# Who issues the modulation weight loads of the first feed-forward and the gate/up product: the GpSimd queue or the weights' queue (SyncE)

## The chip, the cores and the metric

One core of a Trainium2 chip runs the whole program. The metric is device microseconds of one launch. The profile is of one further execution; its times are microseconds from the start of the span. The engines are called PE (TensorE), DVE (VectorE), ACT (ScalarE), POOL (GpSimd) and SP (SyncE, which only issues DMAs here).

## The reference, cut to what matters

Two transformer blocks follow each other on one sequence of 256 tokens, D = 2048, all in float32. Each block has a modulation vector that is a product of one vector with a wide matrix, and the matrix products of a mixer and a feed-forward:

```
mod  = silu(c)   @ w_ada   + b_ada        # first block,  2048 x 12288
mod2 = silu(c_2) @ ada_w_2 + ada_b_2      # second block, 2048 x 12288
...
h = relu(u @ w_ff1)**2 ; y = h @ w_ff2    # first feed-forward,  D_FF = 8192
g = silu(u @ w_gate) * (u @ w_up)         # second one, gate and up, 5632 columns each
```

The modulation needs no TensorE: its matrices (100 MB each) are read chunk by chunk (512 columns) beside the large products and multiplied on DVE.

## The kernel before, in words

`phase_split_product` computes one large product. It runs in turns. In the two products that have an `entry` (first feed-forward, stream "ff_1": 8 turns; gate/up, stream "gate_up": 11 turns) one turn makes two chunks of 512 output columns, and each chunk takes four groups (q = 0 to 3 and q = 4 to 7), a group being four row tiles of weights, 1 MB. Products are exact in float32 by splitting: ACT rounds the weights to a high part (L1108), DVE subtracts it to get the low part (L1187), and PE multiplies high (L1286) and low (L1297).

**The weights' queue.** The ring of weights has two slots of one group, each loaded as two halves of 512 KB by SP (`refill`, L103). The half of group q is asked for when DVE's subtraction has used the same half of group q - 2 (semaphore `used`, raised behind L1187). `load_rest` (L125) is SP's loop over turns and groups.

**The modulation.** The class `Ada` (L195) reads one chunk of a modulation matrix per turn in eight loads of 512 KB (q = 0 to 7) into a ring of four slots that lies in `h_t`. A step (`step`, L254) multiplies one of 16 row tiles on DVE (L273 for the first two, L277 for the rest) and adds to `ada_sums`; behind step 15 one add, one transpose and one reduce follow (L282, L288, L291). A load feeds two steps, 2q and 2q + 1. Steps are laid between the subtractions: in turns from the second on they stand behind the halves of groups 1 to 6, in the proportion 16 steps to 12 places, so that step 14 and 15 stand behind the second half of group 6 and ahead of both subtractions of group 7. In the first turn all 16 stand in groups 4 to 6. In "gate_up" only turns 0 to 3 have steps, in "ff_1" all eight.

The loads are issued by POOL, which has nothing else to do in these phases: four at once, then each as soon as its slot is free (`load_when_free` waits until DVE has done the steps up to 2(q - 3) of that turn, counted by `ada_steps`).

**The end of a chunk.** Behind group 3 and behind group 7, ACT copies the low sums out (L866), DVE adds the high ones (L870), and PE may start the chunk after next in that bank. The first of a chunk's groups and the last are done column tile by column tile, so there PE wants all four row tiles of the group's low parts early; the other groups go row tile by row tile.

Of the kernel before, what the change touches and what calls it, by code (L numbers as in the profile page):

```python
# [22 lines left out]
RING = 2  # L23
# [27 lines left out]
class Chain:  # L51


    def __init__(self, sem):
        self.sem, self.n = sem, 0
# [47 lines left out]
def refill(sp, core, stream, i, q):  # L103

    src = stream.source(i, q)
    ring = core.rows_ring if stream.by_rows else core.ring
    slot, rows = q % RING, src.shape[1] // HALVES
    if isinstance(i, int):
        slot = (stream.first + stream.unit * i + q) % RING
    for half in range(HALVES):  # L110
        if not isinstance(i, int):
            sp.wait_ge(core.used, i * (HALVES * stream.unit) + (HALVES * (stream.first + q - RING) + half + 1))
        elif stream.first + stream.unit * i + q >= RING:
            sp.wait_ge(core.used, HALVES * (stream.first + stream.unit * i + q - RING) + half + 1)
        at = slice(half * rows, (half + 1) * rows)
        sp.dma_start(ring[:, slot, at, 0:src.shape[2]], src[:, at, :]).then_inc(core.landed[slot][half], 16)
# [5 lines left out]
        refill(sp, core, stream, g // stream.unit, g % stream.unit)  # L122


def load_rest(sp, core, stream):  # L125

    if stream.unit % RING == 0:
        with sp.Fori(0, stream.turns - 1) as i:
            for q in range(RING, stream.unit):
                refill(sp, core, stream, i, q)  # L130
            for q in range(RING):
                refill(sp, core, stream, i + 1, q)
        for q in range(RING, stream.unit):
            refill(sp, core, stream, stream.turns - 1, q)
    else:
        for g in range(RING, stream.groups):
            refill(sp, core, stream, g // stream.unit, g % stream.unit)
# [23 lines left out]
ASLOTS = 4  # L161
# [33 lines left out]
class Ada:  # L195
# [1 line left out]

    def __init__(self, ctx, nc, core, parts, turns, slots=ASLOTS, ring=None, acc=None, folded=True, rows=None):  # L200
# [7 lines left out]
        core.ada_landed_n[slots] += turns * self.per_slot  # L208
        core.ada_chunks += turns * self.per_turn
        sb = lambda name, shape: ctx.enter_context(nc.sbuf_tensor(name, shape, F32))  # L210
        self.ring = ring if ring is not None else sb(f"ada_weights_{self.chunks0}", [P, slots, AK, CW])
        self.acc = acc if acc is not None else sb(f"ada_sums_{self.chunks0}", [P, self.per_turn, 2, CW])
        if folded:
            self.folds0 = core.ada_folded
            core.ada_folded += turns * self.per_turn
            self.rows = (rows if rows is not None else
                         sb(f"ada_rows_{self.chunks0}", [P, turns * self.per_turn, NT * P // FOLD]))
            self.groups, at = [], 0
            for which in sorted({which for _, which, _, _ in self.parts}):
                firsts = [chunk0 for _, of, chunk0, _ in self.parts if of == which]  # L220
                self.groups.append((which, min(firsts), len(firsts) * turns, at))
                at += len(firsts) * turns
# [7 lines left out]
    def load(self, queue, i, q):  # L230
        w, _, chunk0, stride = self.parts[q // AGROUPS]
        queue.dma_start(self.ring[:, q % self.slots], w[:, q % AGROUPS, :, bass.ds((i * stride + chunk0) * CW, CW)]
                       ).then_inc(self.landed[q % self.slots], 16)

    def load_when_free(self, queue, i, q):

        steps = KT * self.per_turn
        queue.wait_ge(self.core.ada_steps, i * steps + (KT * self.chunks0 + AK * (q - self.slots + 1)))
        self.load(queue, i, q)

    def first_loads(self, queue):
        for q in range(self.slots):
            self.load(queue, 0, q)

    def other_loads(self, queue):
        n = self.per_turn * AGROUPS
        for load in range(self.slots, self.turns * n):
            self.load_when_free(queue, load // n, load % n)

    def multiply(self, dve, i):  # L250
# [3 lines left out]
    def step(self, dve, i, s):  # L254

        nc, core, n = self.nc, self.core, self.per_turn
# [7 lines left out]
                dve.wait_ge(core.ada_sums_taken, i * n + (self.chunks0 + 1))  # L264
        q = c * AGROUPS + k // AK
        if k % AK == 0:
            dve.wait_ge(self.landed[q % self.slots],
                        i * (16 * self.per_slot) + 16 * (self.landed0 + q // self.slots + 1))
# [721 lines left out]
def phase_split_product(nc, core, name, following, last_step, evictions=None, ada=None, ada_turns=None, entry=None,  # L990
# [7 lines left out]
    st = core.streams[name]  # L998
# [17 lines left out]
    with ExitStack() as ctx:  # L1016
        with_ada = (ada_turns or st.turns) if ada else 0
        ring = None if wide else core.hT[:].rearrange("p a b -> p (a b)").rearrange(
            "p (s k n) -> p s k n", s=ASLOTS, k=AK)
        ada = Ada(ctx, nc, core, ada, with_ada, ring=ring) if ada else None  # L1020
# [61 lines left out]

        @block.sync
        def _(sp):
            load_rest(sp, core, st)
            if following:
                prefetch(sp, core, core.streams[following])

# [265 lines left out]
        if ada:  # L1354
            @block.gpsimd
            def _(pool):
                if ring is not None:

                    pool.wait_ge(core.x_low, KT * (x0 + 1))
                ada.first_loads(pool)  # L1360
                ada.other_loads(pool)
    core.split_groups += st.groups
    core.split_phases += 0 if wide else 1
    core.tiles_ready_n += chunks * signals * st.turns
# [1934 lines left out]
def build(nc, t, out):  # L3299
    with ExitStack() as ctx:  # L3300
        core = Core()
        sb = lambda name, shape, dt=F32: ctx.enter_context(nc.sbuf_tensor(name, shape, dt))
        sem = lambda name: ctx.enter_context(nc.semaphore(name))
# [27 lines left out]
        core.norm_sems = [sem(n) for n in ("squares_ready", "sums_ready", "root_ready")]  # L3331
        core.scaled = sem("input_scaled")
        core.ada_landed = {n: [sem(f"ada_landed_{n}_{s}") for s in range(n)] for n in (IN_1_ASLOTS, ASLOTS, FIRST_ASLOTS)}
        core.ada_landed_n = {IN_1_ASLOTS: 0, ASLOTS: 0, FIRST_ASLOTS: 0}
        core.ada_steps, core.ada_sums_ready, core.ada_sums_taken = (
            sem(f"ada_{n}") for n in ("steps", "sums_ready", "sums_taken"))
# [6 lines left out]
        first = w_ada.rearrange("(g k p) n -> p g k n", p=P, k=KG)  # L3343
# [111 lines left out]
```

## Time and profile before

| what | us |
| --- | --- |
| median of three runs | 2905.76 (2901.91 to 2911.55) |
| the profiled execution, whole | 2904.72 |
| its span in the trace | 2903.0 |
| PE busy in the span | 2751.1 (95%) |
| DVE busy | 2061.6 (71%) |
| ACT busy | 1374.0 (47%) |
| POOL busy | 457.4 (16%) |

The profiled execution's own time is 1.7 us more than its span and 1.0 us less than the median. Stage "ff_1" runs from about 814 to 1192 us, "gate_up" from about 2117 to 2625 us. Busy shares are averages over the whole program; which engine sets the time must be read in each stage. In these two stages TensorE's granted clock is at or near its full level.

### The profile page before, as it was taken

The numbers are of one execution on the slowest core, as the hardware profiler recorded it, in microseconds if no ns is written. First come the engines' busy times: TensorE is split into PE (matmuls) and PEld (weight loads), VectorE is DVE, ScalarE is ACT, GpSimd is POOL, SyncE is SP. The second block draws the span as 40 slices with busy tenths as digits, with TensorE's granted clock in tenths as the row PEclk, the third lists the DMA queues.
The fourth block names the chain that finished last, engine by engine and source line by source line (L and its number), as shares of the span: only waits on it lengthen the run. The fifth ranks groups of instructions, "written<-read, shape, count | busy, mean of one in ns | idle before, by whom it ended". The sixth has DMA issues, their size and how long they took to land. (4 is left out here: it accounts for less than half of the span.)

```text
span 2903.0 us, 49916 instructions
## 1 busy us (share of the span) xinstructions
PE 2751.1 (95%) x19109; PEld 2538.8 (87%) x19109; DVE 2061.6 (71%) x2924; ACT 1374.0 (47%) x2210; POOL 457.4 (16%) x580
## 2 busy tenths in 40 slices
PE   8699999987989999999999999998989999999998
PEld 8689999886878888899998988887878888889998
DVE  6768996786787777787887678786577755555554
ACT  1354446534445555444544455455344444444454
POOL 1002998110011111111111021220011000000000
PEclk6799999998999999999999999999999999999999
DMA  9666666633657788788884666674568755555553
GB/s 386 237 209 241 216 218 197 211 105 130 237 196 273 270 276 277 259 279 282 264 280 134 175 232 221 204 239 135 186 218 279 243 189 186 180 189 166 176 190 129
DMA packets 290937, 632.43 MB, mean 218 GB/s; under 512 B 31490, under 2 KB 52422, under 8 KB 290502
## 3 DMA queue, kind: packets, MB, share of 16 engines
q1 hardware_dynamic: 239120, 484.78, 49.8%
q0 software_dynamic: 40192, 142.63, 14.6%
q10 hardware_dynamic: 11446, 2.54, 0.6%
q8 instruction: 123, 2.02, 0.3%
q14 instruction: 56, 0.46, 0.0%
HBM read 627.77 MB, written 2.10 MB: 217 GB/s over the span
## 5 line engine op out<-in xcount | busy, mean ns | idle before, releaser
L1187 DVE TENSOR_TENSOR weight_parts<-weights,weight_parts 128x1024 fp32r<-128x1024 f32 x584 | 706.9, 1222 | 295.7 <-ACT weight_parts L1108 294.6
L1108 ACT ACTIVATE weight_parts<-weights 128x1024 fp32r<-128x1024 f32 x584 | 607.2, 1057 | 557.0 <-PE accumulators L1297 240.4
L1286 PE MATMUL accumulators<-h_parts,weight_parts 128*128 128x512 f32 x2816 | 778.7, 398 | 20.6 <-DVE h_parts L1174 9.5
L1286 PEld LDWEIGHTS accumulators<-h_parts,weight_parts 128*128 128x128 f32 x2816 | 486.0, 190 | 90.5 <-DVE h_parts L1174 9.8
L1297 PEld LDWEIGHTS accumulators<-h_parts,weight_parts 128*128 128x128 f32 x2944 | 453.4, 190 | 71.0 <-DVE weight_parts L1187 10.5
L1297 PE MATMUL accumulators<-h_parts,weight_parts 128*128 128x256 f32 x2944 | 474.0, 283 | 6.8 <-DVE weight_parts L1187 6.5
L1332 PE MATMUL accumulators<-h_parts,weight_parts 128*128 128x256 f32 x1728 | 436.3, 284 | 1.8 <-DVE weight_parts L1187 1.8
L1334 PE MATMUL accumulators<-h_parts,weight_parts 128*128 128x256 f32 x1728 | 435.8, 284 | 0.0
L1332 PEld LDWEIGHTS accumulators<-h_parts,weight_parts 128*128 128x128 f32 x1728 | 334.1, 193 | 2.3 <-DVE weight_parts L1187 2.3
L1334 PEld LDWEIGHTS accumulators<-h_parts,weight_parts 128*128 128x128 f32 x1728 | 334.0, 193 | 0.0
L1328 PE MATMUL accumulators<-h_parts,weight_parts 128*128 128x256 f32 x1728 | 279.9, 285 | 8.9 <-ACT weight_parts L1108 8.9
L1652 PE MATMUL accumulators<-in_h_parts,in_weight_parts 128*128 128x256 f32 x1024 | 260.5, 287 | 22.9 <-DVE in_weight_parts L1973 22.8
L1654 PE MATMUL accumulators<-in_h_parts,in_weight_parts 128*128 128x256 f32 x1024 | 257.6, 284 | 0.0
L1812 ACT ACTIVATE in_weight_parts<-weights 128x512 fp32r<-128x512 f32 x256 | 157.2, 631 | 203.7 <-PE accumulators L1654 143.6
L1328 PEld LDWEIGHTS accumulators<-h_parts,weight_parts 128*128 128x128 f32 x1728 | 240.1, 193 | 9.3 <-ACT weight_parts L1108 9.3
L1973 DVE TENSOR_TENSOR in_weight_parts<-weights,in_weight_parts 128x512 fp32r<-128x512 f32 x256 | 187.6, 746 | 76.4 <-ACT in_weight_parts L1812 75.7
L2833 PE MATMUL accumulators<-in_h_parts,in_weight_parts 128*128 128x256 f32 x1632 | 216.9, 287 | 9.8 <-DVE in_weight_parts L3218 4.1
L2833 PEld LDWEIGHTS accumulators<-in_h_parts,in_weight_parts 128*128 128x128 f32 x1632 | 203.4, 192 | 21.1 <-issue 8.7
L1652 PEld LDWEIGHTS accumulators<-in_h_parts,in_weight_parts 128*128 128x128 f32 x1024 | 196.9, 192 | 27.6 <-DVE in_weight_parts L1973 27.3
L1654 PEld LDWEIGHTS accumulators<-in_h_parts,in_weight_parts 128*128 128x128 f32 x1024 | 197.2, 193 | 0.0
L2969 ACT ACTIVATE in_weight_parts<-weights 128x512 fp32r<-128x512 f32 (+6 forms) x224 | 120.9, 555 | 153.5 <-PE accumulators L2833 147.2
L3218 DVE TENSOR_TENSOR in_weight_parts<-weights,in_weight_parts 128x512 fp32r<-128x512 f32 (+6 forms) x224 | 129.7, 595 | 74.1 <-ACT in_weight_parts L2969 73.2
(404 smaller groups left out, 3497.3 us busy)
## 6 DMA issues: line engine op xcount, KB each, us to landing
weights<-in_w_ff SPq DMA_DIRECT2D x256, 512.0 KB, 5.4
weights<-in_w_in SPq DMA_DIRECT2D x160, 512.0 KB, 5.1
h_t<-in_ada_w POOLq DMA_DIRECT2D x96, 512.0 KB, 6.4
weights<-in_ffn_w_gate SPq DMA_DIRECT2D x88, 512.0 KB, 4.5
weights<-in_ffn_w_up SPq DMA_DIRECT2D x88, 512.0 KB, 4.6
weights<-in_ffn_w_down SPq DMA_DIRECT2D x88, 512.0 KB, 4.2
weights<-in_w_out SPq DMA_DIRECT2D x64, 512.0 KB, 4.7
wide<-in_ada_w POOLq DMA_DIRECT2D x128, 256.0 KB, 3.9
```

The costliest lines, as they stand in the source:

```text
L1108: nc.scalar.activation(w[:, held:held + take, 0, :], core.ring[:, q % RING, k:k + take, :], ACT.Copy).then_inc(core.high_ready, take)
L1187: ins = nc.vector.tensor_tensor(w[:, held:held + take, 1, :], core.ring[:, q % RING, k:k + take, :], w[:, held:held + take, 0, :].bitcast( ...
L1286: nc.tensor.matmul(core.ps[:, nt, :], high, x[:, kt].rearrange("p a t -> p (a t)"), start=(kt == 0), stop=False, skip_group_check=True)
L1297: ins = nc.tensor.matmul(rest(nt) if two else acc(c, nt), w[:, held, 1, nt * P:(nt + 1) * P], x[:, kt, 0, :], start=False, stop=(kt == KT ...
L1328: nc.tensor.matmul(accs[nt], w[:, held, 0, cols[nt]], xk[:, 0, :], start=(first and nt % 2 == 0), stop=False, skip_group_check=True)
L1332: nc.tensor.matmul(accs[nt], w[:, held, 0, cols[nt]], xk[:, 1, :], start=False, stop=False, skip_group_check=True)
L1334: ins = nc.tensor.matmul(accs[nt], w[:, held, 1, cols[nt]], xk[:, 0, :], start=False, stop=(last and nt % 2 == 1), skip_group_check=True)
L1652: nc.tensor.matmul(acc(c, nt), w[:, k, 0, nt * P:(nt + 1) * P], x[:, kt, 1, :], start=False, stop=False, skip_group_check=True)
L1654: ins = nc.tensor.matmul(acc(c, nt), w[:, k, 1, nt * P:(nt + 1) * P], x[:, kt, 0, :], start=False, stop=(kt == KT - 1 and nt % 2 == 1), sk ...
L1812: nc.scalar.activation(w[:, k, 0, :], core.ring[:, g % RING, part, :], ACT.Copy).then_inc(core.high_ready, 1)
L1973: ins = nc.vector.tensor_tensor(w[:, k, 1, :], core.ring[:, g % RING, part, :], w[:, k, 0, :].bitcast(F32), ALU.subtract)
L2833: ins = nc.tensor.matmul(out, stationary[:, a], moving[:, b], start=(kt == 0 and i == 0 and j == 0), stop=(kt == KT - 1 and i == 2 and j = ...
```

## The change

POOL now issues only the modulation loads of turn 0 of the two products with an `entry`. SP issues those of all later turns: the load q of turn i stands in SP's list right behind the weight refill of the same turn and the same q (both halves). The wait for a free slot is the same one, now done by SP. Landings of SP's loads are counted by four semaphores of their own (`ada_landed_by_sync`), and the DVE steps of turns from 1 on wait for those. SP's loop over turns is cut into pieces, since turn 0, the turns with modulation and those without have different bodies. Other phases are as before.

```diff
-def load_rest(sp, core, stream):
+def load_rest(sp, core, stream, ada=None, ada_turns=0):
+    def loads(i, groups, with_ada):
+        for q in groups:
+            refill(sp, core, stream, i, q)
+            if with_ada:
+                ada.load_when_free(sp, i, q, core.ada_landed_by_sync)
+    def turns(first, end, with_ada, next_with_ada):
+        if first < end:
+            with sp.Fori(first, end) as i:
+                loads(i, range(RING, stream.unit), with_ada)
+                loads(i + 1, range(RING), next_with_ada)
+    last = stream.turns - 1
     if stream.unit % RING == 0:
-        with sp.Fori(0, stream.turns - 1) as i:
...
+        if ada:
+            turns(0, 1, False, True)
+            turns(1, min(ada_turns - 1, last), True, True)
+            if ada_turns <= last:
+                turns(ada_turns - 1, ada_turns, True, False)
+                turns(ada_turns, last, False, False)
+        else:
+            turns(0, last, False, False)
+        loads(last, range(RING, stream.unit), ada is not None and ada_turns == stream.turns)
...
-    def load_when_free(self, queue, i, q):
+    def load_when_free(self, queue, i, q, landed=None):
         steps = KT * self.per_turn
         queue.wait_ge(self.core.ada_steps, i * steps + (KT * self.chunks0 + AK * (q - self.slots + 1)))
-        self.load(queue, i, q)
+        self.load(queue, i, q, landed)
...
         if k % AK == 0:
+            if self.by_sync and not (isinstance(i, int) and i == 0):
+                dve.wait_ge(self.core.ada_landed_by_sync[q % self.slots],
+                            i * (16 * self.per_slot) + 16 * (self.sync0 + q // self.slots + 1 - self.per_slot))
+            else:
...
-            load_rest(sp, core, st)
+            load_rest(sp, core, st, ada if entry else None, with_ada)
...
-                ada.other_loads(pool)
+                ada.other_loads(pool, 1 if entry else None)
```

## Rows read from the trace of the kernel before

**Rows 1.** The page's busy part, and windows of stage ff_1 and of gate_up without modulation.
```profile
PE 2751.1 (95%) x19109; PEld 2538.8 (87%) x19109; DVE 2061.6 (71%) x2924; ACT 1374.0 (47%) x2210; POOL 457.4 (16%) x580
...
core 0: us, PE busy (x) PEld busy (x) DVE busy (x) ACT busy (x) POOL busy (x), PEclk, DMA share, GB/s
890.00:950.00 60.00, 60.00 (x344) 52.43 (x343) 44.53 (x58) 33.97 (x59) 7.36 (x11) 1.00 0.82 286
2310.00:2350.00 40.00, 40.00 (x231) 35.01 (x230) 20.96 (x24) 18.75 (x24) 0.00 (x0) 1.00 0.58 186
```

**Rows 2.** Timeline of ACT: ends of chunks in ff_1 (L909), of turns in gate_up (L960).
```profile
943.49 1.33 ACT L909 ACTIVATE ff_sums<-ff_sums 128x256 f32<-128x256 f32 x4
...
989.34 1.33 ACT L909 ACTIVATE ff_sums<-ff_sums 128x256 f32<-128x256 f32 x4
...
1056.70 1.40 ACT L909 ACTIVATE ff_sums<-ff_sums 128x256 f32<-128x256 f32 x4
...
1079.70 1.33 ACT L909 ACTIVATE ff_sums<-ff_sums 128x256 f32<-128x256 f32 x4
...
2286.82 1.33 ACT L960 ACTIVATE gate<-gate 128x256 f32<-128x256 f32 x4
2332.10 1.33 ACT L960 ACTIVATE gate<-gate 128x256 f32<-128x256 f32 x4
2377.00 1.33 ACT L960 ACTIVATE gate<-gate 128x256 f32<-128x256 f32 x4
```

**Rows 3.** Timeline of PE: idle time in turn 0 and at a chunk's end.
```profile
867.29 0.60 PE L1297 MATMUL accumulators<-h_parts,weight_parts 128*128 128x256 f32 x2 [2.22 <-DVE weight_parts L1187]
...
966.33 1.18 PE L1286 MATMUL accumulators<-h_parts,weight_parts 128*128 128x512 f32 x4 [0.70 <-DVE ff_sums L870]
```

**Rows 4.** Waits of 830 to 1260 us: total, times, longest.
```profile
ACT weight_parts L1108 <- DMA weights<-in_w_ff: 111.2, 56, 4.9
...
DVE ada_sums L277 <- DMA h_t<-in_ada_w: 2.1, 2, 1.9
```

**Rows 5.** Timeline of DVE, one turn of ff_1: group 5's second half to group 7.
```profile
995.35 1.22 DVE L1187 TENSOR_TENSOR weight_parts<-weights,weight_parts 128x1024 fp32r<-128x1024 f32 x1
...
1000.09 1.41 DVE L277 SCALAR_TENSOR_TENSOR ada_sums<-h_t,c_act,ada_sums 128x512 f32<-128x512 f32 x2
1001.53 0.69 DVE L282 TENSOR_TENSOR ada_sums<-ada_sums 128x512 f32<-128x512 f32 x1
...
1003.71 3.49 DVE L1187 TENSOR_TENSOR weight_parts<-weights,weight_parts 128x1024 fp32r<-128x1024 f32 x3
```

**Rows 6.** Timeline of PE: group 7's first low products in that turn.
```profile
1006.63 0.64 PE L1297 MATMUL accumulators<-h_parts,weight_parts 128*128 128x256 f32 x4
```

**Rows 7.** Timeline of POOL (that turn's load q = 7), and L232 from 890 to 1150.
```profile
984.30 0.72 POOL L232 DMA_DIRECT2D h_t<-in_ada_w  x1 [3.98 <-DVE ada_sums L277]
...
L232 POOL DMA_DIRECT2D h_t<-in_ada_w x45: 724/724/724, 893.6 to 1137.0; - x45
```

**Rows 8.** L116 (SP's refills): one issue in that turn; landings from 890 to 1150.
```profile
L116 SPq DMA_DIRECT2D weights<-in_w_ff x1: 373/373/373, 996.7 to 996.7; - x1
...
DMA to landing us min/median/max: 3.6/5.4/9.0
```

**Rows 9.** Three loads in a row on SP's queue, 306 to 308.5 us: L232, L116.
```profile
L232 SPq DMA_DIRECT2D wide<-in_w_ada x1: 379/379/379, 306.1 to 306.1; - x1
...
DMA to landing us min/median/max: 3.9/3.9/3.9
...
L116 SPq DMA_DIRECT2D weights<-in_w_in x2: 327/327/327, 306.7 to 307.5; - x2
...
DMA to landing us min/median/max: 5.0/5.3/5.5
```

**Rows 10.** Timelines of DVE and of PE, the same places of a turn in gate_up.
```profile
2246.70 1.22 DVE L1187 TENSOR_TENSOR weight_parts<-weights,weight_parts 128x1024 fp32r<-128x1024 f32 x1
...
2251.43 1.41 DVE L277 SCALAR_TENSOR_TENSOR ada_sums<-h_t,c_act,ada_sums 128x512 f32<-128x512 f32 x2
...
2259.20 0.64 PE L1297 MATMUL accumulators<-h_parts,weight_parts 128*128 128x256 f32 x4
```

More of the change, by code:

```diff
@@ L122, in prefetch @@
         refill(sp, core, stream, g // stream.unit, g % stream.unit)
-def load_rest(sp, core, stream):
-    if stream.unit % RING == 0:
-        with sp.Fori(0, stream.turns - 1) as i:
[L129 to L134, printed above, removed]
+def load_rest(sp, core, stream, ada=None, ada_turns=0):
[10 more added lines that the diff above has]
+    last = stream.turns - 1
+    if stream.unit % RING == 0:
+        if ada:
[7 more added lines that the diff above has]
+        loads(last, range(RING, stream.unit), ada is not None and ada_turns == stream.turns)
     else:
@@ L195, with __init__ @@
 class Ada:
-    def __init__(self, ctx, nc, core, parts, turns, slots=ASLOTS, ring=None, acc=None, folded=True, rows=None):
+    def __init__(self, ctx, nc, core, parts, turns, slots=ASLOTS, ring=None, acc=None, folded=True, rows=None,
+                 by_sync=False):
+        self.by_sync, self.sync0 = by_sync, core.ada_synced
         self.slots, self.landed, self.folded = slots, core.ada_landed[slots], folded
@@ L207, in __init__ @@
         self.landed0, self.chunks0 = core.ada_landed_n[slots], core.ada_chunks
-        core.ada_landed_n[slots] += turns * self.per_slot
+        core.ada_synced += (turns - 1) * self.per_slot if by_sync else 0
+        core.ada_landed_n[slots] += (1 if by_sync else turns) * self.per_slot
         core.ada_chunks += turns * self.per_turn
@@ L228, in row, with load @@
         return i * stride + (at + chunk0 - first)
-    def load(self, queue, i, q):
+    def load(self, queue, i, q, landed=None):
         w, _, chunk0, stride = self.parts[q // AGROUPS]
         queue.dma_start(self.ring[:, q % self.slots], w[:, q % AGROUPS, :, bass.ds((i * stride + chunk0) * CW, CW)]
-                       ).then_inc(self.landed[q % self.slots], 16)
-    def load_when_free(self, queue, i, q):
+                       ).then_inc((landed or self.landed)[q % self.slots], 16)
+    def load_when_free(self, queue, i, q, landed=None):
         steps = KT * self.per_turn
         queue.wait_ge(self.core.ada_steps, i * steps + (KT * self.chunks0 + AK * (q - self.slots + 1)))
-        self.load(queue, i, q)
+        self.load(queue, i, q, landed)
     def first_loads(self, queue):
@@ L243, in first_loads, with other_loads @@
             self.load(queue, 0, q)
-    def other_loads(self, queue):
+    def other_loads(self, queue, turns=None):
         n = self.per_turn * AGROUPS
-        for load in range(self.slots, self.turns * n):
+        for load in range(self.slots, (turns or self.turns) * n):
             self.load_when_free(queue, load // n, load % n)
@@ L266, in step @@
         if k % AK == 0:
-            dve.wait_ge(self.landed[q % self.slots],
-                        i * (16 * self.per_slot) + 16 * (self.landed0 + q // self.slots + 1))
+            if self.by_sync and not (isinstance(i, int) and i == 0):
+                dve.wait_ge(self.core.ada_landed_by_sync[q % self.slots],
+                            i * (16 * self.per_slot) + 16 * (self.sync0 + q // self.slots + 1 - self.per_slot))
+            else:
+                dve.wait_ge(self.landed[q % self.slots],
+                            i * (16 * self.per_slot) + 16 * (self.landed0 + q // self.slots + 1))
         w = self.ring[:, q % self.slots, k % AK, :]
@@ L1019, in phase_split_product @@
             "p (s k n) -> p s k n", s=ASLOTS, k=AK)
-        ada = Ada(ctx, nc, core, ada, with_ada, ring=ring) if ada else None
+        ada = Ada(ctx, nc, core, ada, with_ada, ring=ring, by_sync=entry is not None) if ada else None
         x = ctx.enter_context(nc.sbuf_tensor(f"h_parts_{g0}", [P, depth if wide else KT, 2, SEQ], F32R))
@@ L3333, in build @@
         core.ada_landed = {n: [sem(f"ada_landed_{n}_{s}") for s in range(n)] for n in (IN_1_ASLOTS, ASLOTS, FIRST_ASLOTS)}
+        core.ada_landed_by_sync, core.ada_synced = [sem(f"ada_landed_by_sync_{s}") for s in range(ASLOTS)], 0
         core.ada_landed_n = {IN_1_ASLOTS: 0, ASLOTS: 0, FIRST_ASLOTS: 0}
```

## The prediction

> **What bounds the kernel now.** I read the page's busy part first, then windows of the two stages that the diff touches, then the ends of chunks one by one. PE is busy 95% of the span, and in a window of ff_1 60.00 of 60 us at the full granted clock; DVE is at 44.53 of 60, and the DMA engines at 0.82 of their time [rows 1]. In gate_up behind the modulation turns PE is also at 40.00 of 40, with the DMA share at only 0.58 [rows 1]. So PE sets the pace with the modulation beside it and without. The ends of chunks say how exactly. A turn without modulation takes 2377.00 - 2332.10 = 44.90 us [rows 2], half a turn 22.45. In ff_1 two half turns run from 943.49 to 989.34, 45.85 us instead of 44.90, and one from 1056.70 to 1079.70, 23.00 instead of 22.45 [rows 2]; the other half turns behind turn 0 are at 22.40 to 22.46. In gate_up one modulation turn takes 45.28 (2286.82 to 2332.10) [rows 2], the other full ones 44.91. What the modulation turns behind turn 0 lose to anything but PE is therefore 0.95 + 0.55 + 0.38 = 1.9 us in all. The first of these shows where it comes from: PE idle 0.70 us, waiting for DVE's eviction of the chunk [rows 3], which was late because its subtractions had waited for weights that had not landed. ACT waited 111.2 us for landings in ff_1, at most 4.9 at a time [rows 4]; nearly all of it is swallowed by the two groups that ACT and DVE run ahead of PE.
>
> **What the change removes.** POOL's issues go: 7 x 8 in ff_1, 3 x 8 in gate_up, each 724 ns [rows 7]. POOL has nothing else here, so that is worth nothing by itself. What can be won is the 1.9 us: before, POOL's loads of a turn come in bunches, just where weights are wanted; behind the change there is one load of 512 KB with every two halves, evenly spread. I take all of the 1.9 as won; the other end is nothing.
>
> The Trainium skill, SBUF — State Buffer, the box "The 'DVE blocks DMA' trap" in the section "SBUF: two separate sides", says that a DVE operation that takes the port pair shared with GpSimd keeps GpSimd from writing its descriptors, and that a load issued from SP is free of this. Here all 45 POOL issues of ff_1 show 724 ns, minimum and maximum alike [rows 7], so the issue itself shows no such wait; the descriptors behind it the trace does not show. By that rule loads would land earlier on SP, which moves nothing beyond what is priced above.
>
> **What it adds on SP.** 24 issues a turn instead of 16, at about 0.37 us each [rows 8]: 8.9 of 44.9 us. The added wait for a free slot never holds SP up, by the order of DVE's list: load q of turn i wants the steps up to 2(q - 3). For q = 4 to 7 these (2, 4, 6, 8 steps) stand behind groups 1, 2 (first half), 3 (first half) and 3, while SP gets there only when the second half of group q - 2 (2, 3, 4, 5) is subtracted; for q = 0 to 3 they are 10, 12, 14 and 16 steps of the turn before, done in its groups 4 to 6, while SP comes behind groups 6, 7, 0 and 1. So nothing queues behind it: the refills stay as early as they are, price 0. If SP did stand still, each microsecond would first eat the lead of some two groups.
>
> **What it moves, and this is the step that costs.** The load is no longer issued when its slot is free, but behind the refill of its own q, and that waits for DVE. For seven of the eight loads there is room: load 6 goes out behind group 4 and is used behind group 5's second half, with the chunk's eviction between (about 9.6 us); the others have that or more. Load 7 has not. Before, it was issued at 984.30 and used by step 14 at 1000.09 [rows 5, 7]: 15.8 us. Behind the change it waits for the second subtraction of group 5, which starts at 995.35 and takes 1.22 [rows 5]. SP's issue of the refill follows at 996.7 [rows 8], and the modulation load behind it at about 997.2 (0.373 for the issue, about 0.1 for registers). Step 14 wants it at 1000.09, 2.9 us later, and the fastest landing of any refill in ff_1 is 3.6 us [rows 8]. So DVE must wait, in every turn from 1 on.
>
> How long: the refill ahead of it lands some 3.5 us behind its issue, since with POOL's loads gone its queue is empty then; the load lands one transfer later. Three loads issued in a row landed at 306.1 + 3.9 = 310.0, at 306.7 + 5.0 = 311.7 and at 307.5 + 5.5 = 313.0 [rows 9]: 1.3 to 1.7 us apart. I take 996.7 + 3.5 + 1.7 = 1001.9, a wait of 1.8 us. From below: 3.6 behind 997.2 is 1000.8, a wait of 0.7. From above: a landing at the 9.0 that ff_1 also shows [rows 8] is 1006.2, a wait of 6.1. The empty queue makes me stay near the lower end.
>
> Behind the waiting step in DVE's list stand steps 14 and 15, the add, the transpose, the reduce, and the two subtractions of group 7. Today the second of those ends at 1003.71 + two thirds of 3.49 = 1006.04 [rows 5]. PE's first low products of group 7 start at 1006.63, the ones of row tile 2 0.27 later, and their weight load 0.2 before [rows 6]: they want it by 1006.7. The slack is 0.65 us, and PE stands for the rest: 1.8 - 0.65 = 1.15 us. It comes back every turn, since DVE and ACT take their next start from PE's end of chunk. The two lost microsecond parts of today don't add to it: group 7's end shifts with PE, so the eviction has more room, not less. ff_1 has 7 such turns: 7 x 1.15 = 8.1 us.
>
> In gate_up the eviction is shorter and DVE earlier. Its second subtraction of group 5 starts at 2246.70, step 14 at 2251.43, 4.73 apart as in ff_1 (1000.09 - 995.35 = 4.74), so the wait is 1.8 again; but step 14 stands 7.77 us ahead of the low products (2259.20) instead of 6.54 (1006.63) [rows 5, 6, 10]. The slack is 0.65 + 1.23 = 1.9, just more than the wait: 3 turns x 0. With a landing 1 us later it would be 3 x 0.9.
>
> **The sum.** 2904.7 - 1.9 + 8.1 = 2910.9; against the median of the runs, 1.0 above the profiled one, the same step of 6.2 us gives 2912. I say 2911, 0.2% above. Turn 0's stall of 2.22 us [rows 3] I leave as it is: there 16 steps stand in three groups and DVE is full; its loads stay with POOL.
>
> The Trainium skill, DMA: Bandwidth & Descriptors, section "SWDGE vs HWDGE vs iDMA", says that an SDMA engine keeps loads issued by GpSimd and by SP in different internal queues and takes turns between them. By that, load 7 loses its own turn when it goes behind the refill in SP's queue; it would land before the refill's end if both queues were used. That is the side my 1.7 us stands on, and no row here compares the two directly.
>
> **Rivals.**
> - Only the relief (the load lands inside the slack). It needs a landing by 1000.09 + 0.65, 3.5 us behind the load's issue with another load just ahead. Then 2904.7 - 1.9 = 2902.8. For it: alone, loads land in 3.6; against it: rows 9. Chance 0.15.
> - More relief: turn 0's stall goes too, because the four POOL loads for turn 1 no longer share its last groups. Then 1.9 + 2.2 in ff_1 + as much in gate_up = 6.3 less: 2898.4. Against it: DVE's list in turn 0 is the same. This is the case on the other side; it decides only if that wait is a landing's. Chance 0.06.
> - Queueing: the refill of group 7 and load 7 find the loads before them still under way, as today's weights do at up to 9.0. A landing at 7.5 behind the refill's issue gives a wait of 4.1, 3.5 on PE in 7 turns and 2.2 in 3: 24.5 + 6.6 - 1.9 = 29, 2934. For it: the share of 0.82 [rows 1]; against: the spread loads. Chance 0.12.
> - SP is held up in a way that the code doesn't show (the pieces of its loop, the issue of 24 loads): refills late by 1 to 2 us in several turns, another 5 to 15 us on the sum, 2920. Chance 0.07. That the slot wait bites is the same case; its order excludes it.
>
> **How the numbers follow.** The forecast's case has 0.60, its own range 2905 to 2918 (waits from 1.2 to 2.7 in ff_1). Within 0.3% is 8.7 us to either side of 2905.8, about what a measurement can tell from no change. Slower by more: a third of the forecast's case (0.20), the queueing case whole, two thirds of SP's: 0.36. Faster by more: 0.05, most of the second rival. Within: 0.59. The range takes the relief in and leaves most of the queueing out: 2900 to 2922.
>
> **What would show it.** In the changed trace: SP issues h_t loads, 56 and 24; the wait of DVE L277 for DMA h_t grows from 2.1 us [rows 4] to some 7 x 1.8 + 3 x 1.8 = 18, once a turn; PE idles about 1.1 us before L1297 at the start of group 7 of ff_1's turns, released by L1187; ends of turns in ff_1 46.0 apart, in gate_up 44.9; ACT's waits for weights in ff_1 well under 111 us. Wrong if DVE does not wait there, if the wait stands elsewhere, or if ff_1's turns are at 44.9.

## The result and the profile after

The changed kernel is slower: median 2919.93 us of 7 runs (2913.27 to 2924.33), the kernel before 2905.4 us of 7 (2901.82 to 2911.55); ratio 1.0049, interval 1.0036 to 1.0063, which is 10 to 18 us. The forecast was 2911, range 2900 to 2922: the place and the mechanism were as written, the loss, 14.5 us, is two to three times the 5 to 6 us forecast. The ratios and intervals in this document are those of the record, not the quotients of the medians given; the two differ by up to 0.001, less than the intervals reach to either side. One of ff1_only's twelve runs, 4419.58 us at a granted clock of 0.55, is counted as a slow one and left out of its ratio.

The page of the changed kernel, its busy part; then its waits from 830 to 1260 us (total, times, longest) and, behind the dots, from 2150 to 2320. Helper lines have moved: L250 issues the modulation loads, L299 is the step, L1209 the low subtraction, L1308 and L1319 the high and low products.

```profile
span 2916.0 us, 49962 instructions
## 1 busy us (share of the span) xinstructions
PE 2756.4 (95%) x19109; PEld 2537.6 (87%) x19109; DVE 2060.9 (71%) x2924; ACT 1375.1 (47%) x2210; POOL 401.1 (14%) x500
```

```profile
ACT weight_parts L1130 <- DMA weights<-in_w_ff: 85.4, 50, 3.9
...
DVE ada_sums L299 <- DMA h_t<-in_ada_w: 17.3, 9, 2.9
PEld accumulators L1319 <- DVE weight_parts L1209: 17.2, 18, 2.7
...
DVE ada_sums L299 <- DMA h_t<-in_ada_w: 7.6, 5, 2.1
```

POOL has 80 instructions fewer: the 56 and 24 loads. PE's busy time is 5.3 us up, its idle time in the span 7.7 us. ACT waits less for weights (85.4 against 111.2 us [rows 4]), and DVE waits more for modulation loads, 17.3 against 2.1 us in the same window.

Where in a turn: the DVE timeline of the changed kernel over the stretch of a turn that [rows 5] show, from group 5's second subtraction to group 7's.

```profile
999.37 1.22 DVE L1209 TENSOR_TENSOR weight_parts<-weights,weight_parts 128x1024 fp32r<-128x1024 f32 x1
1000.51 0.74 DVE L299 SCALAR_TENSOR_TENSOR ada_sums<-h_t,c_act,ada_sums 128x512 f32<-128x512 f32 x1
...
1002.97 1.22 DVE L1209 TENSOR_TENSOR weight_parts<-weights,weight_parts 128x1024 fp32r<-128x1024 f32 x1
1006.48 1.41 DVE L299 SCALAR_TENSOR_TENSOR ada_sums<-h_t,c_act,ada_sums 128x512 f32<-128x512 f32 x2 [2.29 <-DMA h_t<-in_ada_w]
...
1010.10 4.62 DVE L1209 TENSOR_TENSOR weight_parts<-weights,weight_parts 128x1024 fp32r<-128x1024 f32 x4
```

And PE at group 7 of that turn, where [rows 6] show it without idle time:

```profile
1009.73 1.09 PE L1308 MATMUL accumulators<-h_parts,weight_parts 128*128 128x512 f32 x4
1011.37 0.50 PE L1319 MATMUL accumulators<-h_parts,weight_parts 128*128 128x256 f32 x2 [0.55 <-DVE weight_parts L1209]
1012.51 0.51 PE L1319 MATMUL accumulators<-h_parts,weight_parts 128*128 128x256 f32 x2 [0.63 <-DVE weight_parts L1209]
```

The pair of idle times comes back in ff_1's turns 1 to 6 (0.54 to 1.12 us, then 0.63), and in turn 7 one of the two (0.64). The two short idle times add to less than what the turn loses, since the ends of products are modelled; the ends of chunks tell the loss better. Here they are for ACT in the changed kernel, a half turn apart:

```profile
970.91 1.33 ACT L931 ACTIVATE ff_sums<-ff_sums 128x256 f32<-128x256 f32 x4
...
993.37 1.33 ACT L931 ACTIVATE ff_sums<-ff_sums 128x256 f32<-128x256 f32 x4
...
1017.53 1.33 ACT L931 ACTIVATE ff_sums<-ff_sums 128x256 f32<-128x256 f32 x4
```

22.46 us to the end of group 3, as ever, and 24.16 to the end of group 7. Why the wait is 2.3 us and not 1.8, SP's list tells (the changed kernel, the refill of group 7's second half and load 7 behind it in this turn, each with its landing):

```profile
L116 SPq DMA_DIRECT2D weights<-in_w_ff x1: 373/373/373, 1000.8 to 1000.8; - x1
...
DMA to landing us min/median/max: 4.3/4.3/4.3
...
L250 SPq DMA_DIRECT2D h_t<-in_ada_w x1: 372/372/372, 1001.4 to 1001.4; - x1
...
DMA to landing us min/median/max: 5.0/5.0/5.0
```

The refill lands at 1005.1, load 7 at 1006.4, 1.3 us later; DVE starts at 1006.48.

The seven turns differ, and the difference is the best evidence for the mechanism. DVE's waits in turns 1 to 7 are 2.50, 2.41, 2.29, 2.85, 2.28, 2.45 and 1.68 us; the half turns around them take 1.93, 1.82, 1.71, 2.27, 1.70, 1.87 and 1.02 us more than 22.45. Wait less loss is 0.57 to 0.59 us in the first six and 0.66 in the last: each microsecond of wait beyond a slack of 0.6 is one on PE.

**A ledger by stages.** Single executions differ by some us in stages that the change does not touch: the changed kernel's ff_1 had its first chunk's end 3.6 us later in the span than the kernel before. So each kernel is read by three stretches of its own profiled execution: the second half of ff_1's turn 0; ff_1's turns 1 to 7, from that chunk's end to the last one's; and gate_up, from the first chunk's end of turn 0 to that of turn 10. For the kernel before the first two come from these ACT rows, and gate_up from L960 in the same way:

```profile
846.30 1.33 ACT L909 ACTIVATE ff_sums<-ff_sums 128x256 f32<-128x256 f32 x4
...
876.13 1.33 ACT L909 ACTIVATE ff_sums<-ff_sums 128x256 f32<-128x256 f32 x4
...
1191.70 1.32 ACT L909 ACTIVATE ff_sums<-ff_sums 128x256 f32<-128x256 f32 x4
```

| kernel | turn 0, second half | ff_1, turns 1 to 7 | gate_up | ratio to before, interval |
| --- | --- | --- | --- | --- |
| before | 29.83 | 315.57 | 453.23 | |
| changed | 27.45 | 326.57 | 455.41 | 1.0049 (1.0036 to 1.0063) |
| early7 | 27.12 | 314.35 | 452.75 | 0.9985 (0.9971 to 0.9999) |
| early_all | 28.70 | 314.34 | 453.76 | 0.9994 (0.9983 to 1.0006) |
| ff1_only | 27.52 | 326.38 | 453.40 | 1.0034 (1.0022 to 1.0046) |
| gate_only | 27.78 | 315.84 | 455.62 | 0.9992 (0.9981 to 1.0003) |
| pool_late | 26.79 | 325.00 | 453.72 | 1.0041 (1.0026 to 1.0056) |
| steps_to_7 | 23.23 | 314.93 | 449.65 | 0.9975 (0.9965 to 0.9985) |
| pool_steps_to_7 | 23.23 | 315.16 | 449.15 | 0.9973 (0.9961 to 0.9984) |
| best | 23.37 | 314.92 | 448.98 | 0.9976 (0.9966 to 0.9986) |
| late7 | 27.80 | 367.43 | 474.12 | 1.0262 (1.0244 to 1.0280) |

For the changed kernel 11.0 us lie in ff_1's turns 1 to 7. Gate_up has 2.2 more, of which 1.8 are in turn 0 and 0.35 in the turns whose loads SP issues. Turn 0 takes 1 to 3 us more or less in executions of kernels that are alike there, and the granted clock accounts for most of it: DVE's stall makes PE idle, and PE then runs for some time at half its clock, the lower of its two levels, 1.2 GHz. The windows of PE in the kernel before around the stall of [rows 3] (us from:to, length, busy time of PE, PEld, DVE, ACT and POOL, granted clock, DMA share, GB/s), and behind the dots the window of steps_to_7 in which PE idles in the same half turn:

```profile
864.00:867.00 3.00, 1.07 (x6) 0.54 (x4) 2.93 (x4) 1.07 (x2) 0.72 (x1) 1.00 1.05 407
867.00:870.00 3.00, 2.17 (x7) 1.68 (x8) 2.51 (x3) 0.05 (x1) 0.00 (x0) 0.59 1.01 382
870.00:873.00 3.00, 3.00 (x11) 2.52 (x10) 1.89 (x3) 1.67 (x3) 0.00 (x0) 0.50 1.05 387
873.00:876.00 3.00, 3.00 (x16) 2.68 (x15) 0.42 (x1) 0.54 (x2) 0.00 (x0) 0.77 0.82 268
...
873.00:877.00 4.00, 2.83 (x18) 2.27 (x16) 3.97 (x6) 1.19 (x4) 0.00 (x0) 1.00 0.77 261
```

By an estimate, one less the granted clock summed over windows of 1 us, the missing clock is worth 3.4 us in ff_1's turn 0 of the kernel before and 1.7 in the changed one; in gate_up's turn 0 it is 1.7 and 3.4, the other way round. So the 1.8 us of gate_up's turn 0, and most of what ff_1's turn 0 seems to win, come with this clock. Whether the change has a part in it, one execution each can't tell; gate_only, also at 3.4 in gate_up, is over its runs no slower than the kernel before. Besides, the turns of gate_up without modulation take 44.80 us in some executions and 44.90 in others, 0.6 us in its column, which no run explains.

### The profile page after: what moved, and what is told of

The parts are those of the page before. It is cut to its first block and busy times, and to the rows that moved or that the text cites. A ratio compares the mean times of both kernels' runs of the same rounds, so it can differ in the third digit from the quotient of the medians.

```text
span 2916.0 us, 49962 instructions
## 1 busy us (share of the span) xinstructions
PE 2756.4 (95%) x19109; PEld 2537.6 (87%) x19109; DVE 2060.9 (71%) x2924; ACT 1375.1 (47%) x2210; POOL 401.1 (14%) x500
## 3 DMA queue, kind: packets, MB, share of 16 engines
q0 software_dynamic: 28672, 100.68, 10.5%
## 5 line engine op out<-in xcount | busy, mean ns | idle before, releaser
L1209 DVE TENSOR_TENSOR weight_parts<-weights,weight_parts 128x1024 fp32r<-128x1024 f32 x584 | 704.8, 1220 | 272.2 <-ACT weight_parts L1130 270.9
L1308 PE MATMUL accumulators<-h_parts,weight_parts 128*128 128x512 f32 x2816 | 777.9, 398 | 20.6 <-DVE h_parts L1196 9.4
L1308 PEld LDWEIGHTS accumulators<-h_parts,weight_parts 128*128 128x128 f32 x2816 | 485.6, 190 | 90.4 <-DVE h_parts L869 10.1
L1319 PEld LDWEIGHTS accumulators<-h_parts,weight_parts 128*128 128x128 f32 x2944 | 452.8, 190 | 83.4 <-DVE weight_parts L1209 23.6
L1319 PE MATMUL accumulators<-h_parts,weight_parts 128*128 128x256 f32 x2944 | 476.1, 283 | 16.0 <-DVE weight_parts L1209 15.9
L1674 PE MATMUL accumulators<-in_h_parts,in_weight_parts 128*128 128x256 f32 x1024 | 263.6, 289 | 19.0 <-DVE in_weight_parts L1995 18.8
L1676 PE MATMUL accumulators<-in_h_parts,in_weight_parts 128*128 128x256 f32 x1024 | 260.8, 286 | 0.0
L2855 PE MATMUL accumulators<-in_h_parts,in_weight_parts 128*128 128x256 f32 x1632 | 217.7, 288 | 10.5 <-DVE in_weight_parts L3240 5.0
L2855 PEld LDWEIGHTS accumulators<-in_h_parts,in_weight_parts 128*128 128x128 f32 x1632 | 204.1, 193 | 22.2 <-issue 9.1
L1674 PEld LDWEIGHTS accumulators<-in_h_parts,in_weight_parts 128*128 128x128 f32 x1024 | 199.7, 195 | 23.6 <-DVE in_weight_parts L1995 23.4
L1676 PEld LDWEIGHTS accumulators<-in_h_parts,in_weight_parts 128*128 128x128 f32 x1024 | 199.8, 195 | 0.0
L1667 PE MATMUL accumulators<-in_h_parts,in_weight_parts 128*128 128x256 f32 x1024 | 177.9, 297 | 3.7 <-DVE in_h_parts L1865 3.7
```

The source lines that it names most:

```text
L1209: ins = nc.vector.tensor_tensor(w[:, held:held + take, 1, :], core.ring[:, q % RING, k:k + take, :], w[:, held:held + take, 0, :].bitcast( ...
L1308: nc.tensor.matmul(core.ps[:, nt, :], high, x[:, kt].rearrange("p a t -> p (a t)"), start=(kt == 0), stop=False, skip_group_check=True)
L1319: ins = nc.tensor.matmul(rest(nt) if two else acc(c, nt), w[:, held, 1, nt * P:(nt + 1) * P], x[:, kt, 0, :], start=False, stop=(kt == KT ...
L1667: nc.tensor.matmul(acc(c, nt), w[:, k, 0, nt * P:(nt + 1) * P], x[:, kt, 0, :], start=(kt == 0 and nt % 2 == 0), stop=False, skip_group_ch ...
L1674: nc.tensor.matmul(acc(c, nt), w[:, k, 0, nt * P:(nt + 1) * P], x[:, kt, 1, :], start=False, stop=False, skip_group_check=True)
L1676: ins = nc.tensor.matmul(acc(c, nt), w[:, k, 1, nt * P:(nt + 1) * P], x[:, kt, 0, :], start=False, stop=(kt == KT - 1 and nt % 2 == 1), sk ...
```

## The experiments

Each was timed in five rounds beside the kernel before (late7 in three). The diffs are against the changed kernel where nothing else is said.

### early7: one load of eight, one refill earlier

```diff
             refill(sp, core, stream, i, q)
             if with_ada:
-                ada.load_when_free(sp, i, q, core.ada_landed_by_sync)
+                for n in {6: (6, 7), 7: ()}.get(q, (q,)):
+                    ada.load_when_free(sp, i, n, core.ada_landed_by_sync)
```

> The changed kernel, with one load of the eight moved: load 7 of a turn stands behind the refill of group 6 instead of group 7 (SP issues it some 9 us before its use, not 2.9); loads 0 to 6 and the number of loads on SP are as in the changed kernel. Theory 1 (the whole loss is the wait of step 14 for load 7): DVE's wait for h_t loads falls from 23 us to under 4, the half turns of ff_1 that take 24.1 to 24.7 us go back to 22.4 to 22.6, and the time to within 3 us of the kernel before, ratio to it 1.000 (0.999 to 1.001). Theory 2 (SP's queue carries 24 loads of 512 KB a turn and the weights land later for it): DVE's wait goes but PE still waits for subtractions at group 7, and at least half of the 14 us stays, ratio 1.0025 or more.

Measured: 2907.16 us against 2908.69, ratio 0.9985 (0.9971 to 0.9999). DVE's waits for modulation loads in ff_1, of which there is one, in turn 0, and the same stretch of a turn:

```profile
DVE ada_sums L300 <- DMA h_t<-in_ada_w: 0.7, 1, 0.7
```

```profile
1005.05 1.22 DVE L1210 TENSOR_TENSOR weight_parts<-weights,weight_parts 128x1024 fp32r<-128x1024 f32 x1
1006.19 1.41 DVE L300 SCALAR_TENSOR_TENSOR ada_sums<-h_t,c_act,ada_sums 128x512 f32<-128x512 f32 x2
```

Steps 14 and 15 follow the subtraction at once, and all half turns of ff_1 behind turn 0 take 22.45 or 22.46 us: 314.35 for turns 1 to 7, 12.2 less than in the changed kernel and 1.2 less than before. So load 7 alone is the loss. Theory 2 falls: with the same 24 loads a turn on SP's queue PE waits for nothing. The ratio lies below the 0.999 to 1.001 expected; by the medians it is 0.9995, and the interval reaches almost to 1, so that early7 is faster than the kernel before is not shown.

### early_all: every load one refill earlier

```diff
             refill(sp, core, stream, i, q)
-            if with_ada:
-                ada.load_when_free(sp, i, q, core.ada_landed_by_sync)
+            if q + 1 < stream.unit:
+                if with_ada:
+                    ada.load_when_free(sp, i, q + 1, core.ada_landed_by_sync)
+            elif next_with_ada:
+                ada.load_when_free(sp, i + 1, 0, core.ada_landed_by_sync)
```

> The changed kernel, with all modulation loads on SP one refill earlier: load q+1 behind the refill of group q. Theory 1: as with load 7 alone, no wait of DVE for h_t loads over 0.5 us in turns from 1 on, ratio to the kernel before 0.999 to 1.001. The spread loads could also give back the 1.9 us that the turns lost before: then 0.9993. Theory 2 (the weights' landings are what costs): ratio 1.0025 or more.

Measured: 2908.12 against 2908.69, ratio 0.9994 (0.9983 to 1.0006); ff_1's turns 1 to 7 at 314.34, the same as early7. It confirms, and shows that for the other seven loads neither place matters.

### ff1_only and gate_only: the change in one stage

```diff
-        ada = Ada(ctx, nc, core, ada, with_ada, ring=ring, by_sync=entry is not None) if ada else None
+        ada = Ada(ctx, nc, core, ada, with_ada, ring=ring, by_sync=name == "ff_1") if ada else None
...
-            load_rest(sp, core, st, ada if entry else None, with_ada)
+            load_rest(sp, core, st, ada if name == "ff_1" else None, with_ada)
...
-                ada.other_loads(pool, 1 if entry else None)
+                ada.other_loads(pool, 1 if name == "ff_1" else None)
```

(gate_only has "gate_up" in the three places.)

> SP issues the loads of turns from 1 on in ff_1 alone; gate_up is as before. Theory 1: 7 turns at 1.75 us less the 1.5 us that ff_1 lost before, 10 to 12 us over the kernel before, ratio 1.0035 to 1.0045; nearly all of the change's loss. Rival (the loss is the same in each turn of both stages, 14 us over 10 turns): 10 us, so this run alone does not decide, its partner does.

> SP issues the loads of turns from 1 on in gate_up alone (3 turns); ff_1 is as before. Theory 1: DVE waits some 2 us a turn there too but PE's slack of 1.9 us swallows it: 0 to 1 us, ratio 1.000 to 1.0005. Rival (the same loss in each turn): 3 turns at 1.4 to 1.75 us, 4 to 5 us, ratio 1.0015 or more.

Measured: ff1_only 2918.54 against 2908.69 (2918.18 without the run of 4419.58), ratio 1.0034 (1.0022 to 1.0046), a hair under the stretch given, ff_1's turns at 326.38; gate_only 2907.42, ratio 0.9992 (0.9981 to 1.0003), where 1.000 to 1.0005 was expected; the interval holds 1. The loss is ff_1's, though DVE waits in gate_up too: in the changed kernel 1.94, 2.13 and 1.58 us in its three turns, with PE losing 0.35 us in all (0.5 in gate_only). The rival of an equal loss per turn falls; the slack of 1.9 us that the prediction gave that stage is what the runs show.

### pool_late: the old queue, the new moment

Against the kernel before:

```diff
         for load in range(self.slots, self.turns * n):
+            if paced_by and load >= n:
+                queue.wait_ge(self.core.used, HALVES * (paced_by.first + load - RING + 1))
             self.load_when_free(queue, load // n, load % n)
```

> The kernel before (POOL issues all modulation loads), with one more wait ahead of each load of turns from 1 on: the same count of used weights behind which SP issues it in the changed kernel. So the time of issue is the changed kernel's, the queue is the old one. Theory 1 (the time of issue is what costs): DVE waits 2 to 3.5 us at step 14 of each turn, PE loses 1.5 to 3 us in ff_1's seven turns, 12 to 22 us in all, ratio 1.004 to 1.0075. Rival (the place in SP's queue behind a refill costs, and a queue of its own is served at once): the load lands 1 to 1.5 us sooner, waits under 1 us, ratio under 1.0015.

Measured: 2916.65 against 2906.13, ratio 1.0041 (1.0026 to 1.0056). The DVE row of one turn, and POOL's issue of that load 7 with its landing:

```profile
952.23 1.22 DVE L1189 TENSOR_TENSOR weight_parts<-weights,weight_parts 128x1024 fp32r<-128x1024 f32 x1
...
959.04 1.42 DVE L279 SCALAR_TENSOR_TENSOR ada_sums<-h_t,c_act,ada_sums 128x512 f32<-128x512 f32 x2 [1.99 <-DMA h_t<-in_ada_w]
```

```profile
L232 POOL DMA_DIRECT2D h_t<-in_ada_w x1: 722/722/722, 953.7 to 953.7; - x1
...
DMA to landing us min/median/max: 5.2/5.2/5.2
```

ff_1's turns 1 to 7 take 325.0 us, 9.4 over the kernel before; the changed kernel has 11.0 over it. So the moment of issue is 86% of the loss, and who issues at most the rest, 0.2 us a turn. The seven waits at step 14 are 1.9 to 2.6 us, 2.1 in the mean against 2.35 in the changed kernel, and wait less loss is 0.56 to 0.66 us again. The rival asked for a wait under 1 us. The ratio lies within the expectation at its lower end, the 10.5 us between the medians just below its 12 to 22.

From the trigger (952.23 + 1.22) to step 14 it is 5.6 us by POOL, and 5.9 by SP (999.37 + 1.22 to 1006.48). But POOL's load goes out 0.3 us behind the trigger and SP's 0.8 (0.4 in the last turn), since SP issues the refill first; from issue to landing POOL's take 5.1 to 5.8 us in the seven turns and SP's 4.8 to 5.6. The Trainium skill, DMA: Bandwidth & Descriptors, section "SWDGE vs HWDGE vs iDMA", says that the two kinds of queue take turns in a DMA engine. These runs show no gain from that: POOL's load lands earlier by less than it is issued earlier, and what the turns between queues are worth stays open.

### steps_to_7, pool_steps_to_7 and best: no urgent work behind the wait

```diff
             def sums(i, q, k, with_sums):
                 start = 4 if entry and isinstance(i, int) and i == 0 else 1
-                if with_sums and start <= q < st.unit - 1:
-                    n, slots, at = (ada.per_turn * KT, KG * (st.unit - 1 - start) // take,
+                end = st.unit if entry else st.unit - 1
+                if with_sums and start <= q < end:
+                    n, slots, at = (ada.per_turn * KT, KG * (end - start) // take,
```

The same edit on the kernel before is pool_steps_to_7, and on early_all it is best.

> The changed kernel, with DVE's 16 steps laid over groups 1 to 7 instead of 1 to 6 (in turn 0 over groups 4 to 7) in the two products with an entry. The loads and their place in SP's queue are the same; load 7 is then used behind group 7's second half, some 4.5 us later, and nothing that PE wants soon stands behind it. Theory 1: no wait or a harmless one, ff_1's half turns back at 22.4 to 22.6, and in turn 0 of both stages some of the stall of 2.8 us goes too: 3 us over to 6 us under the kernel before, ratio 0.998 to 1.001. Theory 2 (SP's queue delays the weights): ratio 1.0025 or more.

> The kernel before with the same new lay of DVE's steps (over groups 1 to 7, in turn 0 over 4 to 7); POOL issues all modulation loads. It says what that lay gives by itself. Expected: the stalls of turn 0 (2.8 to 3.5 us in each of the two stages) shrink to under 1 us, the rest is as before: 2 to 6 us less, ratio 0.998 to 0.9993. If the last steps now delay the eviction at a turn's end, it is 0 to 5 us slower instead.

> The changed kernel with both repairs: each modulation load one refill earlier on SP, and DVE's steps over groups 1 to 7 (turn 0: 4 to 7). Expected: no wait of DVE for h_t in turns from 1 on, smaller stalls in turn 0, evenly spread loads: 3 to 8 us under the kernel before, ratio 0.997 to 0.999. If the queue of the loads matters apart from their time, it differs from the same lay with POOL's loads by more than 2 us.

Measured: steps_to_7 2898.32, pool_steps_to_7 2897.13, best 2899.43, against 2906.13: ratios 0.9975, 0.9973 and 0.9976, each with an interval of 0.001 to either side. Best is within its expectation; steps_to_7 (0.998 to 1.001) and pool_steps_to_7 (0.998 to 0.9993) are faster than theirs, by more than was said: 7.8 and 9.0 us between the medians, where at most 6 was expected. In steps_to_7 the step stands behind group 7's second subtraction and finds its load landed:

```profile
1003.62 1.23 DVE L1209 TENSOR_TENSOR weight_parts<-weights,weight_parts 128x1024 fp32r<-128x1024 f32 x1 [1.18 <-ACT weight_parts L1130]
1004.76 1.41 DVE L299 SCALAR_TENSOR_TENSOR ada_sums<-h_t,c_act,ada_sums 128x512 f32<-128x512 f32 x2
```

Three things follow. With load 7 at the changed kernel's place in SP's list but used 8.4 us behind its trigger instead of 3.6, the loss is gone (314.93). The lay of the steps is worth 7 to 9 us by itself, nearly all of it in the two turns 0: ff_1's second half falls to 23.23 us from 27 to 30, gate_up's total by 4 us, since 16 steps now stand in four groups instead of three. Two things go there at once: in ff_1 PE's idle time in that half turn falls from 2.5 to 2.9 us in two stalls to 1.1 to 1.3 in one, and the granted clock stays at 1.00, which by the same estimate gives back 1.7 or 3.4 us more; the expectations had priced the idle time alone. And who issues the loads makes no difference that these runs can tell: the three kernels are within 0.0003 of each other. By the medians best is 2.3 us over pool_steps_to_7, a little more than the 2 us that the expectation named as the sign that the queue matters, but that is less than the intervals, 3 us to either side, can tell. All three beat both the kernel before and the changed one; the simplest of them keeps POOL's loads.

### late7: a larger dose

```diff
             refill(sp, core, stream, i, q)
-            if with_ada:
+            if load_7_of is not None and q == 0:
+                ada.load_when_free(sp, load_7_of, 7, core.ada_landed_by_sync)
+            if with_ada and (q < 7 or i is last):
                 ada.load_when_free(sp, i, q, core.ada_landed_by_sync)
```

> The changed kernel with load 7 later still: behind the refill of group 0 of the next turn, about 3.6 us after its place in the changed kernel (the two subtractions of group 6 and the step between them lie in between); in ff_1's last turn, which has no next one, it stays. A dose for the slack. Theory 1 (each microsecond by which load 7 lands beyond the slack is one on PE, once a turn; slack 0.6 us in ff_1, 1.9 in gate_up): DVE waits about 6 us in ff_1's turns 1 to 6 and about 5.5 in gate_up's 1 to 3; PE loses 5.3 in ff_1's six turns, 1.5 in the seventh, and 3.6 in each of the three of gate_up: 44 us over the kernel before, ratio 1.015 (1.012 to 1.018). Rival (PE's two groups of lead take up part of it, the loss saturates): under 25 us, ratio under 1.009.

Measured: 2980.82 against 2906.47, ratio 1.0262 (1.0244 to 1.0280): 74 us over, where 44 were expected. The loss does not saturate; it is more than linear. The DVE row of one turn of late7, then PE's timeline and windows, as above:

```profile
971.09 1.41 DVE L301 SCALAR_TENSOR_TENSOR ada_sums<-h_t,c_act,ada_sums 128x512 f32<-128x512 f32 x2 [7.60 <-DMA h_t<-in_ada_w]
```

```profile
975.97 0.80 PE L1321 MATMUL accumulators<-h_parts,weight_parts 128*128 128x256 f32 x2 [5.86 <-DVE weight_parts L1211]
977.11 0.80 PE L1321 MATMUL accumulators<-h_parts,weight_parts 128*128 128x256 f32 x2 [0.34 <-DVE weight_parts L1211]
977.70 1.91 PE L1310 MATMUL accumulators<-h_parts,weight_parts 128*128 128x512 f32 x4
...
980.26 1.91 PE L1310 MATMUL accumulators<-h_parts,weight_parts 128*128 128x512 f32 x4
...
982.71 1.08 PE L1310 MATMUL accumulators<-h_parts,weight_parts 128*128 128x512 f32 x4
...
984.09 1.09 PE L1310 MATMUL accumulators<-h_parts,weight_parts 128*128 128x512 f32 x4
```

```profile
970.00:976.00 6.00, 0.14 (x2) 0.03 (x1) 4.71 (x7) 0.34 (x1) 0.00 (x0) 0.69 0.09 34
976.00:979.00 3.00, 2.66 (x8) 2.08 (x9) 3.00 (x3) 0.38 (x1) 0.00 (x0) 0.50 0.57 158
979.00:982.00 3.00, 3.00 (x11) 2.52 (x10) 1.08 (x3) 0.38 (x1) 0.00 (x0) 0.50 1.02 358
982.00:985.00 3.00, 3.00 (x17) 2.69 (x16) 0.71 (x2) 1.09 (x4) 0.00 (x0) 0.91 1.04 395
```

Two sizes were off. DVE waits 7.6 us, not 6: the load goes out 3.6 us later behind group 5's subtraction than in the changed kernel, as meant, but in line behind both halves of the next refill, and takes 6.7 us to land, not 5. The six waits are 7.1 to 7.6 us. And PE, idle for 5.9 us, comes back at half its clock: the granted clock is 0.50, the lower of its two levels, 1.2 GHz, and the next two column tiles start 2.56 and 2.45 us apart instead of 1.40, 2.2 us lost. Together 7.6 - 0.6 + 2.2 = 9.2 us; the six half turns concerned lose 7.8 to 9.5, 8.6 in the mean, and gate_up's three turns lose 6.0 to 8.0, where 3.6 was expected. In the changed kernel PE's idle time at this place is 1.2 to 1.8 us in turns 1 to 6 and the granted clock stays at 1.00, so this term was absent there. The Trainium skill, TensorE: Matmul & The Clock Gate, section "Part 1: The HAM clock gate", names the same two levels and puts the drop to the lower one down to idle time; the trace agrees, here behind 5.9 us and in the kernel before's turn 0 behind 2.22 us of idle time.

## Why the prediction was right, and where its sizes were off

- **PE sets the pace; landings of weights are swallowed.** Right. ACT's waits for weights changed from 111 to 85 us and little followed from it (1.2 us, below); the half turns without a late load are at 22.39 to 22.46.
- **Turns behind turn 0 lose 1.9 us before, to be won.** Two thirds right. Of the three parts the 0.95 and 0.55 us in ff_1 are gone in early7 and early_all (turns 1 to 7 at 314.3 against 315.57), 1.2 us by that stretch. The third, 0.38 us in gate_up, was misread: the turn that takes 45.28 us does so in early7, steps_to_7 and ff1_only too. It is the last turn with steps, and PE, which does not idle in it, there does small products that sum the rows (8 in the trace, 0.26 us), work of its own that no load changes.
- **SP's slot wait never bites, 24 issues cost nothing.** Right by early7 and best: SP issues as many loads and waits on the same counts. In the changed kernel SP waited for a free slot three times between 880 and 1200 us, 0.8 us in all.
- **Load 7 is the one that moves from 15.8 us ahead to 2.9.** Right in place and turn: one wait a turn, at step 14, in all ten turns.
- **DVE waits 1.8 us.** This is the mis-sized term. It measured 1.7 to 2.9 us in ff_1's seven turns, 2.35 in the mean. The spacing behind the refill was about right (1.2 to 2.1 us for 1.7); the refill itself was put at 3.5 us, the landing on an empty queue, and took 3.9 to 4.5. The queue is not empty: in the turn shown the refill's first half went out 2.5 us before it, at 998.3, and landed at 1002.2, 1.4 us after the second half's issue.
- **The slack is 0.65 us in ff_1 and 1.9 in gate_up.** Right in ff_1: 2.41 us of waiting cost a half turn 24.27 - 22.45 = 1.82, so 0.6 was slack, and the other turns say the same. Right in gate_up: waits of 1.6 to 2.1 us cost 0.35 in three turns, and wait less loss is 1.8 to 1.9 in the two that lost something.
- **The sum.** 7 x 1.15 = 8.1 us was forecast; seven half turns lost 1.0 to 2.3 us, 1.75 in the mean, 12.2 in all (326.57 - 314.35). Less the 1.2 won, the stretch is 11.0 longer. With the measured wait the prediction's own sum is 7 x 1.7 - 1.5 = 10.4, which the interval of 10 to 18 us holds. The median lies at 14.5 and the stages explain 11; the gap is within the interval, and turn 0's clock alone moves an execution by 1.7 us in either stage. No further mechanism showed. That the range held is in part luck: the median of 2919.93 lies above the 2905 to 2918 of the forecast's own case, whose upper end leaves out what a wait of 2.7 us costs gate_up by the prediction's own slack (3 x 0.8 = 2.4), and inside the 2922 that stood for other cases too.
- **Turn 0 stays.** Its stall is DVE's, as written (in ff_1 a longest idle time of PE of 1.9 to 2.3 us in the traces whose steps stand in three groups; where they stand in four it is gone, and 1.1 to 1.3 us of waiting for the eviction are left, 1.4 to 1.6 in gate_up). The prediction took 2.22 us as its whole size. With the second idle time and the half clock behind it, ff_1's second half of turn 0 is 4.3 to 7.4 us over 22.45 and gate_up's turn 0 3.2 to 5.6 over 44.90; this is where the time of this code lies.
- **The rival of queueing** had a germ of truth in size (landings of 5 us and more), none in extent: at 12% it stood for landings 7.5 us behind the refill, and the changed kernel's seven turns show 5.2 to 6.2.

## What to carry to other kernels

A load that is moved behind a trigger is safe only if the time from the trigger to its use, read off the consumer's list, exceeds a landing on a busy queue, less the slack of what stands behind the use; check every load of the cycle, because one of eight can fail alone. What a late load costs is its wait less the slack of whatever stands behind the waiting instruction in the same list, once per turn, and more once TensorE's granted clock falls; moving the load forward by one trigger or the use back behind the urgent work cured it equally here. Look at the granted clock of a stall before pricing it: by the estimate above the stalls of turn 0 cost 1.7 or 3.4 us more than their idle time in every profiled execution with steps in three groups, but for one, early7's gate_up. Who issues a load mattered 0.2 us a turn here, and when it was issued 1.3 us or more.

## What the runs showed of the hardware

- Loads of 512 KB issued 0.6 us apart on SP's queue landed 1.2 to 2.1 us apart in ff_1's turns 1 to 6 of the changed kernel. There, between 890 and 1150 us at a DMA share of 0.80, landings took 5.4 us in the median for weights and 6.0 for the modulation, where the fastest took 3.7.
- Behind the same trigger a load by GpSimd landed 0.2 us sooner than by SP in the mean of seven turns, though its issue takes 722 ns and not 372; it had gone out some 0.5 us sooner, since SP issued a refill first.
- An idle time of 5.9 us brought TensorE's granted clock to 0.50 and cost 2.2 us on top. So did one of 2.22 us with a second of 0.53 behind it (turn 0 of the kernel before), where the missing clock was worth an estimated 3.4 us; but in early7's gate_up a stall with a longest idle time of 2.25 us left it at 1.00, as pairs of 0.54 to 1.12 and 0.63 us did in the changed kernel's ff_1.
